# Multiplying x by the norm's weights alone ahead of the hybrid layers' products, and each token's factor into the product's bank

## The chip, the core and the metric

The kernel runs on one core of a Trainium2 chip. The metric is device time in microseconds for one launch, median of several runs. PE is the engine of matrix products, DVE and ACT are the vector and scalar engines, POOL is the general one, and SP issues transfers. A bank is one of the eight accumulators that PE writes, [128 partitions x 512 fp32 values].

## The reference, cut

Two transformer layers with a context stream (the first block) are followed by two hybrid layers, each of which computes, on x of 512 tokens by 1024 features:

```python
def rms_norm(x, g):
    xf = x.astype(jnp.float32)
    y = xf * lax.rsqrt(jnp.mean(xf * xf, axis=-1, keepdims=True) + RMS_EPS)
    return (y * g.astype(jnp.float32)).astype(x.dtype)

def hybrid_layer(x, norm_g, w_in, mla_q_a_norm, mla_w_qb, mla_kv_a_norm, mla_w_kvb,
                 mla_q_norm, mla_k_norm, conv_w, swa_q_norm, swa_k_norm, swa_sinks, w_out):
    h = rms_norm(x, norm_g)
    proj = h @ w_in
    ...
    y_mla = mla_mixer(q_lat, kv_lat, k_rope, mla_q_a_norm, mla_w_qb, mla_kv_a_norm,
                      mla_w_kvb, mla_q_norm, mla_k_norm) * jax.nn.silu(g_mla)
    y_conv = short_conv_mixer(c_h, c_b, c_c, conv_w) * jax.nn.silu(g_conv)
    y_swa = swa_mixer(s_q, s_k, s_v, swa_q_norm, swa_k_norm, swa_sinks) * jax.nn.silu(g_swa)
    y = jnp.concatenate([y_mla, y_conv, y_swa], axis=-1) @ w_out
    return x + y
```

`proj` is split into the query and key-value latents of latent attention (256 and 128 columns) with 32 rotary key columns, the queries, keys and values of a banded attention (512, 128, 128), the three inputs of a short convolution (512 each) and three gates (512 each). The norm's factor `lax.rsqrt(...)` is one number for each token, so `(x * g * r) @ w_in` equals `((x * g) @ w_in) * r`, row by row.

## The kernel before

Activations lie with features on partitions and tokens along the free axis, so a tile of the projection is 128 output columns by 512 tokens in one bank (256 tokens in the context stream). Products are in fp32 by three products of split operands for each 128x128 block of weights: `multiply` does w_hi with x_hi (L367), w_hi with x_lo (L368) and w_lo with x_hi (L369). Eight blocks are a chunk of 512 KB, one transfer. Chunks go through four slots; ACT makes w_hi (L345) and DVE w_lo (L353) two chunks ahead of their use, and a slot is loaded again by SP (L310) when its products are done.

The context stage of layer 0 runs from about 45 to 600 us with 256 tokens; the stages of x follow. Stages are blocks: every engine has a program of its own in each, and the next block begins when all have ended. `rest_stage` (L1318) ends the last layer of the first block: after the MLP's last product, ACT squares x (`square`, L910), PE sums in four lanes (`sum`, L918), DVE gathers the sums out of the bank (`gather`, L924), PE folds them to one number for each token (`fold`, L929), ACT takes the root (`root`, L935). `keep_busy` gives PE idle passes (L476) in that wait. Then `load_stage` (L3312) is a block with SP's loads of the hybrid layers' vectors and late constants alone (L3319).

`hybrid_stage` (L4177) begins with `Lead`: DVE inverts the root (`invert`, L940), PE turns it to rows (`turn`, L945: every partition of a bank holds each token's factor), DVE multiplies x by gain and rows (`scaled`, L1008), ACT makes h_hi (L1000), DVE h_lo (L1020), and PE starts the first two tiles' products, which go through the eight pieces of h side by side. Between the first lead operations ACT and DVE also split two chunks.

`Stream` (L3508) holds the tiles after that: ql0, ql1, kv, kpe, sk (the latents, the rotary keys, the banded keys); the second projections of the latents (q, k, v, from `latent_split`); sv, sq0 to sq3, ch and cc by turns, cb0 to cb3; and gated tiles gs, gm, gc, four each. ACT evicts a tile's bank to SBUF (L3618), or for a gated tile takes a tanh of it (L3612), and then DVE multiplies that with the bank again (L3630). `TokenNorms` (L3651) normalizes heads: ACT squares (L3703), PE sums (L3716), root, inverse, turn (L3747), DVE scales (L3763), and for the latents ACT and DVE make `latent_split` (L3774, L3784). `HybridAttention` (L3868) goes in steps of scores (L3933, L3939), row maxima (DVE, L4033, L4035 and L4030), weights (ACT, L3982), row inverse (L4038), turned weights (PE L3965, ACT L3995) and values (L3951). `ShortConv` (L4066) and `OutPair` (L4134, the first two tiles of the out projection) complete it; the last block adds the out projection to x (L4400) and squares it for the norm that follows.

The order of work on each engine is fixed beforehand: every part is a thread that yields a time of a nominal clock, and `weave_by_clock` (L3480) merges them by that time. A product of a block counts 0.64 us, an attention step 2.0; a tile's eviction is marked at the tile's end, DVE's second pass for a gated tile at end + 0.1. An engine waits at each item for its semaphore, and what is marked later stays behind it.

`Core.take` (L412) and `take_high` place tensors in SBUF: those of 16 KB per partition or more at a multiple of 1024 bytes (`LINE`), others at a multiple of 64. In the context stage h_hi is at 65792 and h_lo at 73984, both 256 beyond a multiple of 1024; mid lies over them; merged_hi and merged_lo are at 118208 and 126400, 448 beyond one. The tensors of 512 tokens are at multiples.

## Time and profile before

| | us |
|---|---|
| median of 3 runs | 3624.76 |
| runs | 3621.72, 3632.71, 3624.76 |
| profiled execution | 3623.7 |
| its span | 3621.8 |
| PE busy in it | 3443.0 |
| DVE, ACT busy | 1907.3, 1391.1 |

The span goes from the first instruction to the last. Times in the rows are microseconds from its start. The granted clock is TensorE's, as a share of full speed (2.4 GHz); its other level is half of that. Of a product of 512 columns the row shows 0.39 us or so at full clock, while the next one starts 0.23 us later: matmuls overlap, and the distance of starts is their cost. An idle time in brackets stands before the instruction of its row, with what ended it.

### The profile page before, as it was taken

The page shows a single profiled execution, that of the slowest core. Times are in us where ns is not written, and L with a number is a line of the kernel's source. Part 1 is how long each engine was busy: PE and PEld are TensorE (multiplying, and loading weights), DVE is VectorE, ACT ScalarE, POOL GpSimd, SP SyncE. Part 2 cuts the span into 40 slices and gives each one's busy share as a digit, 9 for nine tenths or more (in the row PEclk, how much of TensorE's full clock was granted, in tenths as well). Part 3 has the DMA queues.
Part 4 walks back from the last instruction along what each step waited for, and adds up shares of the span by engine and source line. Part 5 has one row for each costly group of instructions (what it writes and reads, how often), then busy time and mean ns, then how long its engine had stood idle before and what let it go on. Part 6 is the DMA issues. An engine that isn't in the chain of part 4 may idle for free. (4 is left out here: it accounts for less than half of the span.)

```text
span 3621.8 us, 46539 instructions
## 1 busy us (share of the span) xinstructions
PE 3443.0 (95%) x18460; PEld 2702.2 (75%) x18460; DVE 1907.3 (53%) x3008; ACT 1391.1 (38%) x2381; POOL 72.8 (2%) x58
## 2 busy tenths in 40 slices
PE   7999999999999999998999999999998999989998
PEld 5878898765777677887775677788875776767767
DVE  4755677946544444455856554454443365343653
ACT  3544443244443322234344443322223344343442
POOL 0000000000000000000000000000000000000000
PEclk8999999999999999999999999999998999999999
DMA  5555454211123643334221122223322211222112
GB/s 195 198 196 194 146 185 150 70 59 41 53 65 105 233 159 120 104 94 137 71 70 41 47 70 93 76 90 97 99 88 83 70 61 43 90 93 65 59 41 99
DMA packets 97258, 366.70 MB, mean 101 GB/s; under 512 B 11168, under 2 KB 11424, under 8 KB 95520
## 3 DMA queue, kind: packets, MB, share of 16 engines
q1 hardware_dynamic: 97056, 363.84, 30.4%
q8 instruction: 147, 2.41, 0.3%
q14 instruction: 55, 0.45, 0.0%
HBM read 354.36 MB, written 9.44 MB: 100 GB/s over the span
## 5 line engine op out<-in xcount | busy, mean ns | idle before, releaser
L353 DVE TENSOR_TENSOR w_lo<-w_raw,w_hi 128x1024 fp32r<-128x1024 f32 x545 | 668.9, 1228 | 606.6 <-ACT w_hi L345 606.4
L367 PE MATMUL banks<-h_hi,w_hi 128*128 128x512 f32 (+1 forms) x1960 | 783.2, 400 | 18.7 <-DVE h_lo L1020 6.4
L369 PE MATMUL banks<-h_hi,w_lo 128*128 128x512 f32 (+1 forms) x1960 | 724.9, 370 | 0.0
L368 PE MATMUL banks<-h_lo,w_hi 128*128 128x512 f32 (+1 forms) x1960 | 723.8, 369 | 0.0
L345 ACT ACTIVATE w_hi<-w_raw 128x1024 fp32r<-128x1024 f32 x545 | 573.5, 1054 | 288.6 <-DMA w_raw<-in_stream 277.1
L367 PEld LDWEIGHTS banks<-h_hi,w_hi 128*128 128x128 f32 x1960 | 375.9, 192 | 120.9 <-issue 57.0
L369 PEld LDWEIGHTS banks<-h_hi,w_lo 128*128 128x128 f32 x1960 | 374.9, 191 | 65.1
L368 PEld LDWEIGHTS banks<-h_lo,w_hi 128*128 128x128 f32 x1960 | 376.8, 192 | 59.2 <-issue 11.1
L367 PE MATMUL banks<-merged_hi,w_hi 128*128 128x512 f32 (+1 forms) x960 | 340.8, 355 | 5.1 <-DVE mid L1663 2.3
L369 PE MATMUL banks<-merged_hi,w_lo 128*128 128x512 f32 (+1 forms) x960 | 337.5, 352 | 0.0
L368 PE MATMUL banks<-merged_lo,w_hi 128*128 128x512 f32 (+1 forms) x960 | 337.5, 352 | 0.0
L367 PE MATMUL banks<-mid_hi,w_hi 128*128 128x512 f32 (+1 forms) x768 | 274.5, 357 | 0.9 <-DVE y L1680 0.5
L369 PE MATMUL banks<-mid_hi,w_lo 128*128 128x512 f32 (+1 forms) x768 | 271.7, 354 | 0.0
L368 PE MATMUL banks<-mid_lo,w_hi 128*128 128x512 f32 (+1 forms) x768 | 271.7, 354 | 0.0
L367 PEld LDWEIGHTS banks<-merged_hi,w_hi 128*128 128x128 f32 x960 | 180.3, 188 | 42.0 <-issue 7.1
L1870 ACT ACTIVATE turned<-banks 128x512 f32<-128x512 f32 (+1 forms) x176 | 96.7, 549 | 283.2 <-PE banks L1849 283.1
L369 PEld LDWEIGHTS banks<-merged_hi,w_lo 128*128 128x128 f32 x960 | 180.3, 188 | 25.3
L368 PEld LDWEIGHTS banks<-merged_lo,w_hi 128*128 128x128 f32 x960 | 180.4, 188 | 24.4
L1594 ACT ACTIVATE mid_hi<-mid 128x512 fp32r<-128x512 f32 (+1 forms) x96 | 54.0, 562 | 309.8 <-DVE mid L1663 309.8
L367 PEld LDWEIGHTS banks<-mid_hi,w_hi 128*128 128x128 f32 x768 | 145.1, 189 | 32.5 <-issue 5.4
L2642 DVE SCALAR_TENSOR_TENSOR branch<-conv_in,vectors,branch 128x512 f32<-128x512 f32 (+1 forms) x270 | 168.1, 670 | 0.2
L369 PEld LDWEIGHTS banks<-mid_hi,w_lo 128*128 128x128 f32 x768 | 145.2, 189 | 20.2
(389 smaller groups left out, 4729.4 us busy)
## 6 DMA issues: line engine op xcount, KB each, us to landing
w_raw<-in_stream SPq DMA_DIRECT2D x545, 512.0 KB, 3.5
mod_cells<-in_stream SPq DMA_DIRECT2D x48, 512.0 KB, 5.4
mod_cell<-in_stream SPq DMA_DIRECT2D x48, 512.0 KB, 5.4
x_kept<-x SPq DMA_DIRECT2D x3, 2048.0 KB, 7.2
x<-x_kept SPq DMA_DIRECT2D x3, 2048.0 KB, 9.9
x<-in_x SPq DMA_DIRECT2D x2, 2048.0 KB, 8.3
out_x<-x SPq DMA_DIRECT2D x8, 256.0 KB, 4.3
dft_table<-in_dft SPq DMA_DIRECT2D x2, 768.0 KB, 5.6
```

What stands on the lines that cost most here:

```text
L345: self.nc.scalar.activation(self.hi[:, c], self.raw[:, c], ACT.Copy).then_inc(self.hi_ready, 1)
L353: self.nc.vector.tensor_tensor(self.lo[:, c], self.raw[:, c], self.hi[:, c].bitcast(F32), ALU.subtract)\
L367: self.nc.tensor.matmul(out, w_hi, x_hi, start=start, stop=False)
L368: self.nc.tensor.matmul(out, w_hi, x_lo, start=False, stop=False)
L369: mm = self.nc.tensor.matmul(out, w_lo, x_hi, start=False, stop=stop)
L1594: nc.scalar.activation(mid_hi[:, t], m[:, t % 2], ACT.Copy).then_inc(mid_hi_ready.sem, 1)
L1870: nc.scalar.activation(self.T[:, lane:lane + lanes, a:b, i * P:(i + 1) * P], K.ps[:, 4, 0:lanes * (b - a) * P].rearrange("p (l k n) -> p l ...
L2642: nc.vector.scalar_tensor_tensor(out=self.out[:, c], in0=src, scalar=w, in1=self.out[:, c], op0=ALU.mult, op1=ALU.add).then_inc(self.done. ...
```

## The change

Ahead of a hybrid layer, `GainLead` takes the place of `Lead`. It multiplies x by the gain only (ACT to hi, DVE to lo), without a wait for the norm's factor. Gather, fold, root, invert and turn are taken out of the end of the stage before and done by the new lead beside the first pair's products: gather first on DVE, fold on PE after piece 0, root on ACT after hi tile 3, invert on DVE after lo tile 4, turn on PE after piece 4. ACT copies the rows to SBUF. Two calls of `keep_busy` go with the fold.

Each tile that uses all eight pieces of h (`raw`) is multiplied on DVE, in its bank, by those rows, at the tile's end; ACT's eviction is marked 0.2 later and waits for that (`normed`), and DVE's second pass of a gated tile is marked 0.3 after the end.

The loads of `load_stage` are issued by SP in the last `rest_stage`, behind its last weight load; the late constants go in space that `branch` gives back early.

`half_skip` is 448 while the context stage is built: split tensors of 8 to 16 KB are then placed 448 beyond a multiple of 1024. With it h_hi is at 65984 and h_lo at 74176; merged stays 448 beyond one, and branch_hi and branch_lo, which were at 448 and 320, come to 448. It is None again for the stages of x.

```diff
--- before.py
+++ after.py
...
     LINE = 1024
+    half_skip = None
...
+    def line_of(self, size, dt):
+        if size >= 16 * self.LINE:
+            return self.LINE, 0
+        if size % self.LINE or size < 8 * self.LINE or self.half_skip is None or dt != F32R:
+            return 64, 0
+        return self.LINE, self.half_skip
+
     def take(self, name, shape, dt=F32):
         size = -(-4 * int(np.prod(shape)) // 64) * 64
-        step = self.LINE if size >= 16 * self.LINE else 64
-        at = -(-self.low // step) * step
+        step, skip = self.line_of(size, dt)
+        at = -(-(self.low - skip) // step) * step + skip
...
+class GainLead:
...
+    def ready(self, pe, k):
+        pe.wait_ge(self.lo_ready.sem, self.lo_ready.at(k + 1))
+
+    def wait_rows(self, eng):
+        eng.wait_ge(self.rows_out.sem, self.rows_out.at(1))
+
+    def pe_beside(self, pe, k):
+        if k == 0:
+            self.norm.fold(pe)
+        elif k == self.n // 2:
+            self.norm.turn(pe)
...
+    def act(self, act, chunks):
+        nc, W = self.K.nc, self.K.W
+        for k in range(self.n):
+            nc.scalar.activation(self.hi[:, k, 0:self.NT], self.src[:, k, 0:self.NT], ACT.Copy, scale=self.gain[:, k:k + 1])\
+                .then_inc(self.hi_ready.sem, 1)
+            if k == self.n // 2 - 1:
+                self.norm.root(act)
+        for c in chunks:
+            W.split_hi(act, c)
+        self.norm.wait_rows(act)
+        nc.scalar.activation(self.rows, self.norm.rows, ACT.Copy).then_inc(self.rows_out.sem, 1)
+
+    def dve(self, dve, chunks):
+        nc, W = self.K.nc, self.K.W
+        self.norm.gather(dve)
+        for k in range(self.n):
+            dve.wait_ge(self.hi_ready.sem, self.hi_ready.at(k + 1))
+            nc.vector.scalar_tensor_tensor(out=self.lo[:, k, 0:self.NT], in0=self.src[:, k, 0:self.NT],
+                                           scalar=self.gain[:, k:k + 1], in1=self.hi[:, k, 0:self.NT].bitcast(F32),
+                                           op0=ALU.mult, op1=ALU.subtract).then_inc(self.lo_ready.sem, 1)
+            if k == self.n // 2:
+                self.norm.invert(dve)
+        for c in chunks:
+            W.split_lo(dve, c)
...
+        @block.sync
+        def _(sp):
+            for dst, src in loads:
+                sp.dma_start(dst, src).then_inc(vectors_in.sem, 16)
+            if loads:
+                sp.wait_ge(vectors_in.sem, vectors_in.at(16 * len(loads)))
...
-                K.keep_busy(pe, busy // 8, 0)
-                following.fold(pe)
...
-                following.root(act)
...
-            if following is not None:
-                following.gather(dve)
...
+        if loads_of is not None:
+            K.give(branch)
...
+        self.normed, self.raw = K.count_of("stream_normed"), [t for t, tile in enumerate(tiles) if len(tile.ks or ()) == KD]
...
-            yield self.end(t)
-            self.wait_done(act, t)
+            yield self.end(t) + (0.2 if t in self.raw else 0.0)
+            if t in self.raw:
+                self.wait_normed(act, t)
+            else:
+                self.wait_done(act, t)
...
+            if t in self.raw:
+                yield self.end(t)
+                if t == self.raw[0]:
+                    self.lead.wait_rows(dve)
+                self.wait_done(dve, t)
+                nc.vector.tensor_tensor(self.out(t), self.out(t), self.lead.rows[0:tile.cols], ALU.mult)\
+                    .then_inc(self.normed.sem, 1)
             if tile.gate:
-                yield self.end(t) + 0.1
+                yield self.end(t) + 0.3
...
+        lead.norm.sq = K.over("lead_squares", temps, F32, [4, NT])
...
-            lead.pe(pe)
             for k in range(KD):
                 lead.ready(pe, k)
                 for t in range(2):
                     W.multiply(pe, K.ps[:, t, 0:NT], first + t * KD + k, h[0][:, k], h[1][:, k], k == 0, k == KD - 1)
+                lead.pe_beside(pe, k)
...
-                following.fold(pe)
...
-            if following is not None:
-                following.root(act)
...
-            lead.dve(dve, lead.squares, range(split - AHEAD, split))
+            lead.dve(dve, range(split - AHEAD, split))
...
-            if following is not None:
-                following.gather(dve)
...
+        hybrid_vectors = []
+
+        def hybrid_loads():
+            K.late_consts = K.take_high("late_consts", [CONST_N - N_EARLY])
+            hybrid_vectors.append(K.take("vectors_2", [2, VEC2_N]))
+            return [(hybrid_vectors[0][:, n], A["vec2"][n]) for n in range(2)] + [(K.late_consts[:], A["consts"][:, N_EARLY:])]
...
+                K.half_skip = 448
...
+            K.half_skip = None
...
-        K.late_consts = K.take("late_consts", [CONST_N - N_EARLY])
...
-        load_stage(K, [(vec2[:, l], A["vec2"][l]) for l in range(2)] + [(K.late_consts[:], A["consts"][:, N_EARLY:])],
-                   "vectors_in")
...
-            lead = Lead(K, before, x, vec[:, VEC2_AT["norm_g"]:VEC2_AT["norm_g"] + 8], None, h[0], h[1], SEQ, False)
+            lead = GainLead(K, before, x, vec[:, VEC2_AT["norm_g"]:VEC2_AT["norm_g"] + 8], h[0], h[1], SEQ)
```

## Rows read from the trace of the kernel before

**Rows 1.** The page: span, and busy time by engine.

```profile
span 3621.8 us, 46539 instructions
...
PE 3443.0 (95%) x18460; PEld 2702.2 (75%) x18460; DVE 1907.3 (53%) x3008; ACT 1391.1 (38%) x2381; POOL 72.8 (2%) x58
```

**Rows 2.** Windows: stretch, length, busy us by engine, TensorE clock, DMA share, GB/s.

```profile
2732.00:2752.00 20.00, 16.58 (x61) 13.54 (x62) 13.43 (x21) 8.19 (x12) 0.00 (x0) 0.73 0.37 135
2946.00:2980.00 34.00, 33.19 (x194) 22.57 (x193) 21.58 (x76) 19.02 (x49) 0.00 (x0) 1.00 0.20 63
3040.00:3070.00 30.00, 27.34 (x171) 20.41 (x168) 16.29 (x35) 13.77 (x33) 0.00 (x0) 1.00 0.12 36
3180.00:3200.00 20.00, 15.93 (x61) 13.07 (x62) 13.46 (x21) 8.51 (x13) 0.00 (x0) 0.75 0.37 134
45.00:150.00 105.00, 98.43 (x764) 93.83 (x764) 83.40 (x166) 55.28 (x102) 4.52 (x6) 0.96 0.44 140
460.00:570.00 110.00, 109.20 (x925) 108.14 (x923) 83.76 (x130) 51.87 (x67) 0.00 (x0) 1.00 0.58 182
```

**Rows 3.** Timeline ahead of hybrid layer 1: start, length, engine, line, operation, idle before.

```profile
2704.91 0.34 SPq L310 DMA_DIRECT2D w_raw<-in_stream  x1
...
2722.75 0.69 DVE L924 COPY squares<-banks 128x512 f32<-128x512 f32 x1 [3.37 <-PE banks L918]
...
2723.49 1.05 PE L929 MATMUL banks<-consts,squares 128*128 128x1 f32 x8 [0.24 <-DVE squares L924]
...
2725.17 0.82 SPq L3319 DMA_DIRECT2D vectors<-in_vec  x2
...
2732.20 2.08 PE L945 MATMUL banks<-consts,norm 128*128 128x128 f32 x8 [7.66 <-DVE norm L940]
...
2735.31 1.40 DVE L1008 SCALAR_TENSOR_TENSOR scaled<-x,vectors,banks 128x512 f32<-128x512 f32 x2
...
2737.49 0.80 PE L367 MATMUL banks<-h_hi,w_hi 128*128 128x512 f32 x1 [3.22 <-DVE h_lo L1020]
```

**Rows 4.** Timeline ahead of hybrid layer 2.

```profile
3176.99 1.28 ACT L935 ACT_TABLE_LOAD   x1
...
3178.16 0.69 DVE L924 COPY squares<-banks 128x512 f32<-128x512 f32 x1 [1.85 <-PE banks L918]
...
3180.60 2.00 ACT L345 ACTIVATE w_hi<-w_raw 128x1024 fp32r<-128x1024 f32 x2 [0.34 <-PEq L4192]
...
3186.15 0.80 PE L367 MATMUL banks<-h_hi,w_hi 128*128 128x512 f32 x1 [3.21 <-DVE h_lo L1020]
```

**Rows 5.** Timeline of PE in the context stage: products on h, then on merged.

```profile
121.52 0.28 PE L367 MATMUL banks<-h_hi,w_hi 128*128 128x256 f32 x1
...
121.88 0.28 PE L367 MATMUL banks<-h_hi,w_hi 128*128 128x256 f32 x1
...
400.01 0.28 PE L367 MATMUL banks<-merged_hi,w_hi 128*128 128x256 f32 x1
...
401.03 0.28 PE L367 MATMUL banks<-merged_hi,w_hi 128*128 128x256 f32 x1
```

**Rows 6.** Timeline of the hybrid layers: pair ends, squares, the out pair.

```profile
2750.58 1.28 ACT L3618 ACTIVATE latents<-banks 128x512 f32<-128x512 f32 x2 [4.77 <-PE banks L369]
...
2756.46 1.78 PE L3716 MATMUL banks<-consts,token_squares 128*128 128x1 f32 x8 [3.88 <-ACT token_squares L3703]
...
2770.00 1.26 PE L3716 MATMUL banks<-consts,token_squares 128*128 128x1 f32 x6 [1.86 <-ACT token_squares L3703]
...
3097.51 0.50 PE L367 MATMUL banks<-swa_out_hi,w_hi 128*128 128x512 f32 x1 [4.11 <-DVE gate_conv L3630]
...
3198.53 1.28 ACT L3618 ACTIVATE latents<-banks 128x512 f32<-128x512 f32 x2 [4.07 <-PE banks L369]
```

**Rows 7.** Instructions of line 4400.

```profile
L4400 DVE TENSOR_TENSOR x<-x,banks x16: 680/686/689, 3124.1 to 3618.6; 128x512 f32<-128x512 f32 x16
```

**Rows 8.** Waits from 2946 to 3102: us in total, times, longest.

```profile
ACT weights L3982 <- DVE neg_max L4035: 30.1, 13, 3.0
```

More of the change, by code:

```diff
@@ L427, in take_high @@
         size = -(-4 * int(np.prod(shape)) // 64) * 64
-        step = self.LINE if size >= 16 * self.LINE else 64
-        at = (self.high - size) // step * step
+        step, skip = self.line_of(size, dt)
+        at = (self.high - size - skip) // step * step + skip
         for a, b, _ in sorted(self.held, key=lambda h: -h[0]):
@@ L432, in take_high @@
                 break
-            at = min(at, (a - size) // step * step)
+            at = min(at, (a - size - skip) // step * step + skip)
         assert at >= self.low, (name, size)
@@ L1315, in close, with rest_stage @@
             self.K.give(t)
-def rest_stage(K, x, merged, mod, mods, NT, following, gates, h, kept, M=None, homes=(), fetch=None, side=None, ahead=None):
+def rest_stage(K, x, merged, mod, mods, NT, following, gates, h, kept, M=None, homes=(), fetch=None, side=None, ahead=None, loads=()):
     nc, W = K.nc, K.W
@@ L1689, in _ @@
                 wait_added(dve, 1, by_pool[-1])
[L1690 to L1691 removed]
+    vectors_in.advance(16 * len(loads))
     residuals = 1 if late_chain else 2
@@ L3453, in block_one_stream @@
     if M is None:
-        late = rest_stage(K, x, merged, mod, mods, NT, after, gates, h, kept, side=side_of() if side_of is not None else None)
+        if loads_of is not None:
+            K.give(branch)
+        late = rest_stage(K, x, merged, mod, mods, NT, after, gates, h, kept, side=side_of() if side_of is not None else None, loads=loads_of() if loads_of is not None else ())
     else:
@@ L3468, in block_one_stream @@
         h = ()
-    for t in (branch, y_hi) + h + merged:
+    for t in ((branch, y_hi) if loads_of is None else (y_hi,)) + h + merged:
         K.give(t)
@@ L3633, in close @@
     def close(self):
-        for s, n in ((self.evicted, len(self.tiles)), (self.gated, len(self.gates)), (self.tile_done, self.done)):
+        for s, n in ((self.evicted, len(self.tiles)), (self.normed, len(self.raw)), (self.gated, len(self.gates)), (self.tile_done, self.done)):
             s.advance(n)
```

28 lines of the change are left out of this document (19 added, 9 removed).

## The prediction, made before the change was built

> **What bounds the kernel now.** The first view is the page's head: PE is busy 3443.0 us of a span of 3621.8, DVE 53% of it, ACT 38% [rows 1]. So PE's products set the time, and an edit pays where it closes a hole in PE's row, or makes a product shorter, and costs where it opens a hole. The profiled execution took 3623.7 us (1.9 around the span) and the median of the runs is 3624.76, 1.1 more; my sum is made on 3623.7. The windows view [rows 2] shows where PE has holes: 3.4 and 4.1 us of 20 at the start of the two hybrid layers (with a granted clock of 0.73 and 0.75), little in the first attention stretch (33.19 of 34), more in a later one (27.34 of 30); in the context stretches PE is busy 94% and 99%. The timeline [rows 3, 4] shows the joints ahead of the hybrid layers, and the waits what the products wait for behind them.
>
> **Part 1: the joint before hybrid layer 1.** DVE gathers the last sums at 2722.75, PE folds at 2723.49, the vectors are loaded from 2725.17, and the next block begins only as they have landed, its turn at 2732.20; two splits, scaled, hi and lo follow, and the first product starts at 2737.49 [rows 3]. After the change the loads are issued behind the last weight load of the stage before (2704.91), 17 us ahead of that gather; SP has nothing queued behind them but its wait for them, and from issue to the next block's first work they took 7.0, so they are covered; were they not, the joint would give up to 7 less. The next block begins about 2723.1 (the sum's arrival at DVE plus the 0.34 that PE's sequencer took at the same joint of layer 2 [rows 4]). A hi tile on ACT and a lo tile on DVE are one operation each on 128x512 from SBUF, for which I take L1008's 0.70; the gather (0.69) runs beside the first hi. First product: 2723.1 + 0.70 + 0.70 = 2724.5, or 13.0 earlier. The four passes of L476 that go lay beside the gather: nothing. The pair of tiles is 48 products. Before they last 2737.49 to 2750.5 [rows 3, 6], 13.0, in which DVE's 1.4 us per k and a low clock are the pace. After, ACT and DVE need 0.70 per k and PE 6 x 0.227 = 1.36 (0.227 being twice the 113.3 ns of 256 columns in [rows 5]), so PE is the pace: 10.9, plus the fold 1.05 and the turn now in its midst, 2.08 at the low clock and half at full: 13.0. The pair ends at 2738.2, with 0.7 for a clock not yet full: 12.3 us gained (11.3 to 13).
>
> **Part 2: the joint before layer 2.** There is no load here. Gather 3178.16, block 3180.60, first product 3186.15, pair's end 3198.53 [rows 4, 6]. After: block 3178.5, first product 3179.9, pair 13.0, and 1.9 more since PE has just idled and the clock is low here before: 3194.8. Gained 3.7 (2.5 to 5). The root's table load (1.28), now beside the sums, falls between ACT's hi tiles 3 and 4, where ACT is 2 us ahead of PE: nothing. Both joints: 16.0.
>
> **Part 3: one multiply more per tile.** 34 tiles in each layer take all 8 pieces of x (5 first ones, sv, 4 sq, 4 ch, 4 cc, 4 cb, 12 gates). Each has its bank multiplied on DVE before ACT may evict it. The like operation is L4400, a TENSOR_TENSOR that adds a bank into 128x512: 0.686 us [rows 7]; with the signal I take 0.74. 34 x 0.74 = 25.2 us of DVE in each layer, and DVE is free 37% and 46% of the two attention stretches [rows 2]; the price is not DVE's time but what waits in ACT's and PE's written-out order. ACT's eviction now stands behind DVE's queue; behind it on ACT stand squares and w_hi splits, and PE waits for the squares' sum.
> - ql pair: PE idles 3.88 for the squares now, which come behind a split that waits for its transfer; the multiply hides under that wait: 0.
> - kv, sk: PE idles 1.86 for kv's squares [rows 6], so nothing covers the delay. kv's multiply stands behind the latents' lo steps on DVE: +1.7; sk +0.75.
> - sv, sq0, ch0, cc0 (the first tile behind another kind): 0.65 to 0.75 each, 2.9 together; sq1, sq2 0.45 together, since norms come later there by the order.
> - cb: the convolution's steps are queued on DVE ahead of the multiply: 1.5 + 1.4 + 0.8, and 0.6 at the first attention step: 4.3.
> Sum 10.1 per layer; I take 9.5 for some overlap, with 5 (only the uncovered ones) and 11 as bounds.
>
> **Part 4: the multiply among the attention.** The 12 gated tiles end while DVE and ACT pass scores to and fro: ACT waits 30.1 us for neg_max in 13 places [rows 8]. A multiply put ahead of a neg_max delays it, ACT's weights, the turn and then PE. By the kernel's own clock the attention goes in steps of 2 us and gated tile t (0 to 11) ends at 5.12 x (t + 1), so its phase in a step is that modulo 2. At phases 0.24 to 0.48 (tiles 1, 3, 10) the multiply is written right ahead of the step's neg_max, and DVE waits there for the tile's last product too: 1.8 each, 5.4. At 0.08, 1.2, 1.36 and 1.84 (tiles 8, 9, 2, 6) it delays the rescaling of weights by its own length or so: 3.2. At the others it falls where DVE waits for ACT: 0. Sum 8.6, an estimate from 0.74 and the order of the code. PE has next to no hole early (0.8 in 34 us) and 2.7 in 30 later, which means the chain has some slack early and none later. I take 8 per layer, bounds 3 (only the later tiles pay) and 10. The gates' second pass (L3630) goes from 0.1 to 0.3 behind the tile's end and has ACT's tanh ahead of it now as before; who needs it (gates, gate_conv) comes later: in the same price. The 4.11 us for which PE waits for gate_conv ahead of the out pair [rows 6] stays: the tanh there stands behind a w_hi split that outlasts the multiply.
>
> **Part 5: the clock.** More holes on PE may mean more stretches at the low clock, as the first products of each layer have. Such a stretch costs about its length less half: I add 1.5 in all (0 to 4).
>
> **Part 6: where h, mid and branch lie in the context stage.** With the skip of 448, h_hi and h_lo of 256 columns move from 256 to 448 beyond a multiple of 1024 bytes, and mid over them as well; merged is at 448 now. Nobody else moves but branch. In the trace products on h_hi start every 120 ns (121.52 to 121.88 in three) and on merged_hi and merged_lo every 113.3 (400.01 to 401.03 in nine), both at full clock, with weight tiles of the same size [rows 5]. 1416 products on h and 768 on mid would gain 2184 x 6.5 ns = 14.2 us, and PE is 94 to 99% busy there [rows 2], and transfers take 0.44 to 0.58 of their engines' time there, so what products lose in length the end mostly gains. I take 12.5; bounds 0 (the gap is due to something else) and 14.5.
> The Trainium skill has a rule that speaks against this part. Its page "TensorE: Matmul & The Clock Gate", section "Wait — 56ns, not 53.3ns?", gives the start-to-start distance as the columns by the clock and about 2.5 ns, and section "Step-by-step: what each phase is for" has cycles by the number of columns alone: where the operand begins isn't in it. By it this part is worth nothing, and the sum would be rival D's. The trace does not agree as it stands, since the two distances above differ at one size and one clock; that placement is the reason is not shown by it.
>
> **Sum.** -16.0 (joints) -12.5 (placement) +2 x (9.5 + 8.0) = +35.0 +1.5 (clock) = +8.0: 3623.7 to 3631.7 profiled, 3632 on the median. What measurement can tell from no change is about 0.3%, 10.9 us: below 3613.9 is faster, above 3635.6 slower.
>
> **The rivals.**
> - A (forecast): gains and costs nearly cancel. 3632, its own range 3621 to 3642.
> - B (slower): the multiply is never covered, since DVE's, ACT's and PE's order is fixed and each tile's eviction hands its delay on. Price 34 x 0.74 = 25.2 per layer, 50.3 in place of 35: -16 -12.5 +50.3 +1.5 = +23.3, 3648. It decides once more than 19.4 us per layer reach PE (26 of the 34 tiles). For it: the kv and sk sums stand bare already. Against: PE's 33.19 of 34 with DVE only 63% busy; where PE is the pace, a later eviction delays nobody.
> - C (faster): DVE's free time takes the multiply except at kv, sk and the first tiles of a kind (5 per layer), and in the attention only the later tiles pay (3): 2 x 8 = 16: -16 -12.5 +16 = -12.5, 3612. For it: early attention is PE's. Against: the 30 us in which ACT waits on DVE.
> - D (the placement does not do it): costs as in A, no gain in the context stage: 3644.5.
> - That the front gains nothing (the loads land late, or the first k waits for the turn after all) I hold below 1 in 20; the code hands PE the first tiles without the norm factor.
>
> **How the numbers follow.** Chances: A 0.52, B 0.12, C 0.26, D 0.10. Faster: half of C, 0.13. Slower: B, four fifths of D and a quarter of A, 0.33. The rest is within 0.3%: 0.54. The range takes all of A, D, most of C and the near part of B: 3610 to 3646.
>
> **What would show it.** The pair's end (ACT's first latents) at about 2738 in place of 2750.58, and about 3.7 gained over the second joint. Products on h_hi at 113 ns in place of 120, and the x stages starting 12 us earlier. PE's hole at kv's sum 3.5 in place of 1.86; each hybrid layer from its pair's end to its last product longer by 17 us. I am wrong if that length grows by under 8 (C) or over 23 (B), or if h stays at 120 (D).

## The result, and the profile after

The changed kernel takes 3659.55 us (median of 5, 3652.36 to 3667.54) against 3624.7 for the kernel before (5 runs): ratio 1.0094, interval 1.0083 to 1.0104. It is 34 us slower, by 0.9%; the forecast was 3632 with a range to 3646. The profiled execution has a span of 3657.8, 36.0 more than [rows 1].

The page of the kernel after, its first lines:

```profile
span 3657.8 us, 46573 instructions
...
PE 3451.7 (94%) x18456; PEld 2700.9 (74%) x18456; DVE 1941.4 (53%) x3060; ACT 1393.1 (38%) x2383; POOL 74.1 (2%) x58
```

PE has 8.7 us more of busy time and 36 more of span. To find where they arise, the products of both kernels (13032 in each, in one order) are set side by side: the start of each tile's first product after, less the same product's start before, and how that difference grows. In both profiled executions:

| from, to | before | after | grows by | forecast |
|---|---|---|---|---|
| start to the first product at 784 (context stage over) | 784.1 | 780.1 | -4.0 | -12.5 |
| to layer 1's first product | 2737.49 | 2720.43 | -13.1 | -13.0 |
| to its kv tile (the pair is done) | 2751.06 | 2736.51 | +2.5 | +0.7 |
| to its gs1 (tiles ahead of the gates) | 2955.74 | 2957.53 | +16.3 | +9.5 |
| to its last product (attention, out projection) | 3175.20 | 3187.24 | +10.3 | +8 |
| to layer 2's first product | 3186.15 | 3192.15 | -6.0 | } -3.7 |
| to its kv tile | 3199.01 | 3208.23 | +3.2 | } |
| to its gs1 | 3400.02 | 3424.99 | +15.8 | +9.5 |
| to its last product | 3618.16 | 3654.13 | +11.0 | +8 |

The sum is +36.0. The joints gave 13.4 and not 16.0, the placement 4.0 and not 12.5, and the layers behind their first pairs took 53.3 more and not 35.0.

The 53.3 are of two kinds. The windows view tells them apart, as PE does the same instructions in both kernels between two such products (stretch, length, busy us of PE, PEld, DVE, ACT, POOL, clock, DMA share, GB/s). Before, the context stage and layer 1 from kv to gs1 and from gs1 to its last product:

```profile
47.95:784.10 736.15, 706.75 (x4995) 622.23 (x4995) 496.66 (x839) 330.50 (x554) 16.73 (x18) 0.99 0.46 152
...
2751.06:2955.74 204.68, 193.12 (x985) 151.18 (x984) 83.32 (x135) 77.67 (x137) 14.59 (x9) 0.96 0.22 68
2955.74:3175.20 219.46, 204.25 (x1141) 151.93 (x1139) 107.06 (x259) 92.65 (x213) 0.00 (x0) 0.99 0.20 65
```

After, the same three:

```profile
48.20:780.10 731.90, 702.26 (x4995) 616.51 (x4995) 496.71 (x839) 330.15 (x554) 17.25 (x18) 0.98 0.47 153
...
2736.51:2957.53 221.02, 198.90 (x985) 153.16 (x984) 97.51 (x157) 78.03 (x137) 15.00 (x9) 0.94 0.20 63
2957.53:3187.24 229.71, 206.17 (x1140) 152.79 (x1139) 114.95 (x271) 93.42 (x213) 0.00 (x0) 0.99 0.19 62
```

From kv to gs1 PE is idle (length less busy) 22.1 us where it was 11.6, and busy 198.90 where it was 193.12, for the same 985 instructions. Over both layers PE's idle time grows by 38.5 us, against 35.0 forecast for the multiplies, and its busy time by 14.8, where the forecast had 1.5 for the clock. The length of a product depends on the granted clock, and one place in layer 1 shows it (before, then after):

```profile
2922.00:2926.00 4.00, 3.79 (x23) 2.99 (x22) 4.00 (x7) 1.38 (x3) 0.00 (x0) 1.00 0.27 104
...
2922.00:2926.00 4.00, 3.81 (x15) 3.18 (x16) 3.22 (x7) 0.40 (x2) 0.00 (x0) 0.63 0.02 4
```

Before, the clock is 1.00 there. After, it is 0.63, products of 512 columns start 0.43 us apart and not 0.23, and PE has just been idle for 2.79 us (timeline, PE):

```profile
2922.19 1.10 PE L3795 MATMUL banks<-consts,token_squares 96*128 96x1 f32 x8 [2.79 <-ACT token_squares L3782]
```

So a hole in PE's row costs its own length, and behind some holes a stretch at the lower clock follows and costs more. Which holes do that is not shown.

In the context stage PE's idle time is the same (29.6 for 29.4) and its busy time 4.5 us shorter.

The timeline of the kernel after ahead of layer 1 answers [rows 3] (start, length, engine, line, operation, idle before it):

```profile
2701.39 0.81 SPq L1462 DMA_DIRECT2D vectors<-in_vec  x2
...
2718.89 0.69 DVE L932 COPY lead_squares<-banks 128x512 f32<-128x512 f32 x1 [3.72 <-PEq L1403]
...
2720.43 0.50 PE L367 MATMUL banks<-h_hi,w_hi 128*128 128x512 f32 x1 [2.01 <-DVE h_lo L1094]
...
2721.73 0.63 PE L369 MATMUL banks<-h_hi,w_lo 128*128 128x512 f32 x1
...
2722.16 1.70 PE L937 MATMUL banks<-consts,lead_squares 128*128 128x1 f32 x8
...
2736.84 1.20 ACT L3690 ACTIVATE latents<-banks 128x512 f32<-128x512 f32 x2 [3.63 <-DVE banks L3704]
```

The loads are out at 2701.39, the block begins at 2718.9 and the first product comes 1.5 later, as forecast. But from 2721.73 the products are longer (0.63 for 0.40), the fold (L937) takes 1.70 in place of 1.05, and PE's clock is low, 0.66 over 2720 to 2730:

```profile
2720.00:2730.00 10.00, 9.57 (x32) 7.91 (x33) 7.56 (x12) 6.03 (x10) 0.00 (x0) 0.66 0.65 238
```

Layer 2's joint, for [rows 4, 6]:

```profile
3192.15 0.50 PE L367 MATMUL banks<-h_hi,w_hi 128*128 128x512 f32 x1 [2.01 <-DVE h_lo L1094]
...
3208.56 1.20 ACT L3690 ACTIVATE latents<-banks 128x512 f32<-128x512 f32 x2 [3.65 <-DVE banks L3704]
```

Measured from the last product of layer 1, the first of layer 2 comes 6.0 sooner than before, and 3.2 are given back while the pair runs, as in layer 1 (2.5).

Who pays for the multiply is told by its own line, all 68 of them (lengths ns, what DVE idled for ahead of it, and who waited for it, us and times):

```profile
L3704 DVE TENSOR_TENSOR banks<-banks,lead_rows x68: 674/694/700, 2736.1 to 3574.5; 128x512 f32<-128x512 f32 x66, 96x512 f32<-96x512 f32 x2
...
  PE banks L369: 42.5, 24
...
  ACT conv_b L3690: 49.7, 8
  ACT swa_q L3690: 40.5, 8
...
  ACT gates L3684: 9.6, 8
```

It lasts 0.694 us against the 0.686 of [rows 7]. DVE stood idle 42.5 us in front of 24 of them until PE had finished the tile, and ACT's evictions stood idle for the multiply: 49.7 us for the 8 of conv_b. Most of that is no price. Before, ACT was idle ahead of the same 8 evictions too, until PE had finished the tile:

```profile
  PE banks L369: 36.6, 8
```

The growth is 13.1 us, 1.6 for each eviction, and 8.4 for the 8 of swa_q (40.5 for 32.1), 1.05 each. Ahead of the gates' tanh, where ACT never idled before, it is 9.6 us now for gates and as much for gate_conv. So an eviction is late by more than the 0.69 of its multiply.

How that reaches PE in the attention is seen at one gate, gs3. Before (timeline, lines of ACT and DVE):

```profile
2986.38 0.58 ACT L3612 ACTIVATE gates<-banks 128x512 f32<-128x512 f32 x1
...
2986.85 1.05 ACT L345 ACTIVATE w_hi<-w_raw 128x1024 fp32r<-128x1024 f32 x1
...
2988.49 0.17 DVE L4030 TENSOR_SCALAR neg_max<-row_max 128x2 f32<-128x2 f32 x1
...
2988.70 0.51 ACT L3982 ACTIVATE weights<-with_bias,neg_max 128x257 f32<-128x257 f32 x1 [0.79 <-DVE neg_max L4030]
...
2989.70 0.57 ACT L3995 ACTIVATE turned<-banks 128x512 f32<-128x512 f32 x1
```

After, the same gate:

```profile
2992.51 0.17 DVE L4109 TENSOR_SCALAR neg_max<-row_max 128x2 f32<-128x2 f32 x1
2992.59 0.69 DVE L3704 TENSOR_TENSOR banks<-banks,lead_rows 128x512 f32<-128x512 f32 x1
...
2992.71 0.51 ACT L4061 ACTIVATE weights<-with_bias,neg_max 128x257 f32<-128x257 f32 x1 [2.23 <-DVE neg_max L4109]
...
2993.71 0.57 ACT L3684 ACTIVATE gates<-banks 128x512 f32<-128x512 f32 x1
...
2994.19 1.04 ACT L345 ACTIVATE w_hi<-w_raw 128x1024 fp32r<-128x1024 f32 x1
...
2995.14 0.58 ACT L4074 ACTIVATE turned<-banks 128x512 f32<-128x512 f32 x1
...
2995.77 0.44 PE L4030 MATMUL banks<-turned,swa_values 128*64 128x128 f32 x4 [0.78 <-ACT turned L4074]
```

Before, ACT waits for DVE's neg_max (the negated row maximum that the weights need) in any case, and does the tanh (L3612) and a w_hi split in that time: 1.6 us for nothing, with 0.79 of idleness left. After, the tanh (L3684) needs the multiply (L3704), which DVE does only behind both with_bias and neg_max. So ACT idles 2.23 ahead of the weights, and the tanh and the split come between the weights and `turned`, on the path: `turned` starts 2.43 behind the weights, where it was 1.00, and PE waits for it. From gm0, in which this falls, to gm1 the difference grows by 1.77.

Distances of products in the context stage, for [rows 5]. On merged, in two stretches of the kernel after:

```profile
359.15 0.28 PE L367 MATMUL banks<-merged_hi,w_hi 128*128 128x256 f32 x1
...
359.86 0.28 PE L367 MATMUL banks<-merged_hi,w_hi 128*128 128x256 f32 x1
...
404.17 0.28 PE L367 MATMUL banks<-merged_hi,w_hi 128*128 128x256 f32 x1
...
404.51 0.28 PE L367 MATMUL banks<-merged_hi,w_hi 128*128 128x256 f32 x1
```

0.71 us for six (118 ns) in the first, 0.34 for three (113) in the second, at one address and one clock. Over the whole stage, of products of 256 columns that follow one another directly at full clock, those on h start every 115.4 ns on average (119.4 before), on mid every 114.0 (119.8) and on merged every 114.3 (113.7). With branch that is 3.0 ns for each of some 3200 products, or 9.6 us.

### The profile page after: what moved, and what is told of

Read it like the earlier page. It is cut to its first block and busy times, and to the rows that moved or that the text cites. A ratio compares the mean times of both kernels' runs of the same rounds, so it can differ in the third digit from the quotient of the medians.

```text
span 3657.8 us, 46573 instructions
## 1 busy us (share of the span) xinstructions
PE 3451.7 (94%) x18456; PEld 2700.9 (74%) x18456; DVE 1941.4 (53%) x3060; ACT 1393.1 (38%) x2383; POOL 74.1 (2%) x58
## 5 line engine op out<-in xcount | busy, mean ns | idle before, releaser
L368 PEld LDWEIGHTS banks<-h_lo,w_hi 128*128 128x128 f32 x1960 | 378.2, 193 | 60.0 <-issue 11.3
```

The lines of the kernel that those rows point to most:

```text
L368: self.nc.tensor.matmul(out, w_hi, x_lo, start=False, stop=False)
```

## The experiments

All times are medians, and the ratios are to runs of the kernel before made beside them (medians of 3626.4 to 3627.0 there). Each edit is shown in part; "..." marks what is left out. From one profiled execution of each kernel, the table gives the growth of the difference to before in the stretches above (B: kv to gs1, C: gs1 to the last product, of layers 1 and 2), and PE's idle time in them, as length less busy time.

| kernel | us | ratio, interval | at kv, layer 1 | B1 | C1 | B2 | C2 | PE idle in B1, C1, B2, C2 |
|---|---|---|---|---|---|---|---|---|
| before | | | 0 | 0 | 0 | 0 | 0 | 11.6, 15.2, 11.3, 15.2 |
| after | 3659.6 | 1.0094 (1.0083 to 1.0104) | -14.6 | 16.3 | 10.3 | 15.8 | 11.0 | 22.1, 23.5, 22.4, 23.6 |
| e1_placement_only | 3620.8 | 0.9983 (0.9973 to 0.9992) | -1.1 | -0.5 | -0.2 | 3.1 | -0.1 | 11.6, 15.3, 11.6, 15.2 |
| e2_no_multiply | 3612.3 | 0.9960 (0.9946 to 0.9974) | -20.9 | -1.7 | 2.1 | 3.7 | 0.7 | 11.5, 15.8, 11.7, 15.8 |
| e3_plain_only | 3646.2 | 1.0051 (1.0034 to 1.0068) | -14.2 | 16.2 | 0.6 | 20.2 | 4.2 | 22.3, 15.8, 22.3, 15.8 |
| e4_one_column | 3646.2 | 1.0049 (1.0032 to 1.0066) | -13.0 | 8.4 | 8.1 | 14.0 | 11.9 | 16.4, 20.7, 16.5, 19.4 |
| e5_loads_placement | 3615.0 | 0.9956 (0.9939 to 0.9972) | -9.4 | -0.1 | 0.1 | 3.2 | 0.0 | 11.5, 15.3, 11.5, 15.2 |
| e6_late_marks | 3671.6 | 1.0121 (1.0104 to 1.0138) | -14.7 | 16.2 | 13.9 | 20.4 | 13.8 | 22.3, 22.7, 22.3, 22.0 |
| e7_pool | 3632.4 | 1.0016 (1.0006 to 1.0025) | -14.3 | -3.5 | 12.9 | 1.9 | 12.0 | 12.6, 22.7, 12.6, 23.6 |
| e8_offset_0 | 3632.3 | 1.0011 (1.0001 to 1.0021) | 11.2 | -0.1 | 0.0 | 0.3 | 0.0 | 11.5, 15.2, 11.6, 15.2 |
| e9_dve_beside | 3622.4 | 0.9992 (0.9982 to 1.0001) | -10.6 | -0.2 | 6.2 | 0.1 | 6.1 | 12.6, 18.7, 12.7, 18.6 |
| e10_act_waits_dve | 3627.0 | 1.0001 (0.9991 to 1.0010) | -14.6 | -1.9 | 10.3 | 5.2 | 8.5 | 12.5, 20.9, 12.7, 20.9 |
| e11_pool_no_gates | 3611.5 | 0.9959 (0.9946 to 0.9972) | -15.1 | 3.1 | 0.6 | 5.1 | 2.3 | 12.6, 15.8, 12.6, 15.8 |
| e12_pool_gates | 3605.2 | 0.9942 (0.9925 to 0.9959) | -13.3 | 2.8 | -3.2 | 5.0 | -3.5 | 12.4, 12.4, 12.6, 12.3 |

The idle time repeats within 0.4 us where kernels have the same work in a stretch (B of before, e1, e2, e5 and e8, both layers of after). The growth does not: with no multiply in B it still moves by 5 us from one execution to another (e2, e5, e11), in steps of about 1.6 at kv, kpe, sk and gs0. These steps are the clock: in B2, e1 is 3.1 us longer than before at 0.3 more of idle time, and its granted clock is 0.96 for 0.97. So the idle time tells the waits, and the rest of the growth is PE's busy time at a lower or higher clock. Over B and C of both layers PE is busy 790 us in before, 790 to 798 in all the kernels in which DVE multiplies no tile outside the gates but kpe, and 805 to 818 in after, e3, e4 and e6, in which it does. So more low clock comes with those multiplies, by more than executions differ. With the gates' alone (e7) it doesn't: 795.

**e1_placement_only.** The placement alone.

```diff
+                K.half_skip = 448
                 late = block_one_stream(K, c, vec, lam[:, l], mod[:, 1], mods[:, 1], CTX, kv_c, [kv_c], None, A["dft256"],
...
+            K.half_skip = None
             x = block_one_stream(K, x, vec, lam[:, l], mod[:, 0], mods[:, 0], SEQ, kv_x, [kv_x, kv_c], A["rope"],
```

> The kernel before, with the placement of the context stage alone (half_skip 448). Theory taken (products get shorter, but part of that is given back in longer waits ahead of products): 4 us faster than before, 3620 to 3622, with products on h and mid starting every 113 to 118 ns. Rival (all that products lose in length the end gains): 8 us or more faster, 3616 or less. Rival (placement does nothing, the 4 us seen by 784 us are chance): within 1 us of before.

3620.8, 6.2 less than before (3 to 10 by the interval): the placement is worth something, and less than the forecast's 12.5. The two ends expected, 4 and 8, both lie in the interval. It is a firmer measure than the -4.0 of one execution: in the twelve profiled kernels with this placement the first product at 784 comes between 9.2 us earlier than before (e2) and 0.4 later (e9), 3.1 earlier on average.

**e8_offset_0.** The same with 0 in place of 448.

```diff
-                K.half_skip = 448
+                K.half_skip = 0
```

> The kernel before with the context stage's split tensors of 8 to 16 KB placed at 0 beyond a multiple of 1024 bytes in place of 448 (merged too, which before was at 448). If the offset alone sets the distance of products: 120 ns or more on h, mid and merged alike, merged 6.7 ns slower than before, and 960 x 6.7 ns = 6.4 us at most to lose: 3627 to 3633. If it is another property of the addresses that made h slow (distance to the weights' slots, or overlap with what others read): h or mid at 114 ns in some stretch, or merged still at 113.

Its timeline of PE, on merged:

```profile
420.00 0.28 PE L367 MATMUL banks<-merged_hi,w_hi 128*128 128x256 f32 x1
...
420.72 0.28 PE L367 MATMUL banks<-merged_hi,w_hi 128*128 128x256 f32 x1
```

0.72 for six: 120 ns, where the same tensor 448 beyond a multiple started every 113.3 in [rows 5]. All through the stage h, mid and merged are at 119 to 120 in this kernel. 3632.3 is 4 to 5 us over before (0 to 8 by the interval), and 6.4 at most was expected. With the h of before (256 beyond) at 120 and of after at 113 to 118, three offsets of the streamed operand are told apart with all else equal: 0 and 256 are slow, 448 is fast. That the offset sets the distance is shown by merged, which moved from 448 to 0 and became slower; why is not shown, and neither is why 448 gives 113 in some stretches and 118 in others.

**e5_loads_placement.** The kernel before with placement and the moved loads, its own `Lead` kept.

```diff
+            for dst, src in loads:
+                sp.dma_start(dst, src).then_inc(vectors_in.sem, 16)
...
-        load_stage(K, [(vec2[:, l], A["vec2"][l]) for l in range(2)] + [(K.late_consts[:], A["consts"][:, N_EARLY:])],
-                   "vectors_in")
```

> The kernel before with the placement and with the loads moved into the last stage of the first block, and with its own Lead, norm and evictions: the parts of the change that add no multiply. Theory: the block that only loads (about 7 us) goes whole, since the loads are covered: 6 + 7 = 13 us faster than before, 3612 to 3616, the first product of hybrid layer 1 starting 7 us earlier and the layers as long as before. Rival (the loads take room in the queue or in SP's order and delay the last stage): 3618 or more.

```profile
2720.27 0.69 DVE L932 COPY squares<-banks 128x512 f32<-128x512 f32 x1 [3.37 <-PE banks L926]
...
2722.71 2.00 ACT L345 ACTIVATE w_hi<-w_raw 128x1024 fp32r<-128x1024 f32 x2 [0.34 <-PEq L1351]
...
2728.26 0.79 PE L367 MATMUL banks<-h_hi,w_hi 128*128 128x512 f32 x1 [3.30 <-DVE h_lo L1028]
```

From gather to first product are 8.0 us here and 14.7 in [rows 3]: 6.7 less, so the loads' block goes whole. 3615.0, 12 under before (10 to 22 by the interval). Of the 13.1 that the changed kernel gains at this joint, 7 are the loads and 6 the new lead, which gives 2.5 back in the pair.

**e2_no_multiply.** The changed kernel with no multiply: both layers lack the norm factor.

```diff
-        self.normed, self.raw = K.count_of("stream_normed"), [t for t, tile in enumerate(tiles) if len(tile.ks or ()) == KD]
+        self.normed, self.raw = K.count_of("stream_normed"), []
```

> The changed kernel with no tile multiplied by the tokens' factor, and evictions waiting for the tile's last product as before: it leaves out the norm factor of both hybrid layers. Theory (the multiply costs all that each layer lost behind its first pair, 26.5 us): 3659.5 - 53 = 3606, and each layer from kv to its last product as long as before. Rival (a part of the loss comes with the new lead itself, its splits and its copy, not with the multiply): 3612 or more, with the loss left ahead of the sk tile.

3612.3: 47 of the 53 go by the medians, at the rival's 3612. But what the rival says, a loss left ahead of sk by the new lead itself, isn't found: PE's idle time in B is that of before (11.5 and 11.7), and only 0.6 in each C is left. The multiply and its waits cause the loss. This kernel is also the most that this lead could give with the places of all else kept, 14.5 us under before, and no better than e5, which keeps the old lead and is complete.

**e3_plain_only.** The multiply at all tiles but the gates, which lack the factor.

```diff
-        self.normed, self.raw = K.count_of("stream_normed"), [t for t, tile in enumerate(tiles) if len(tile.ks or ()) == KD]
+        self.normed, self.raw = K.count_of("stream_normed"), [t for t, tile in enumerate(tiles) if len(tile.ks or ()) == KD and not tile.gate]
```

> The changed kernel with the multiply at the 22 tiles per layer that are not gates, and none at the 12 gated ones: the gates lack the norm factor. If the prices add: 3659.5 - 2 x 11 = 3637.5, with the attention stretch as long as before. If the delay of one part is taken up by the other (a tile that comes late leaves slack for the next): the gain is under 15, 3645 or more.

3646.2, 13.4 less and not 22. In waits the prices add: PE's idle time in C falls to that of e2 (15.8), and in B it stays that of after (22.3). The time doesn't follow in full since the clock differs: C2 is 4.2 and B2 20.2 here, at the same idle time as in e2 and after. So the expectation of 22 and the rival's "under 15" were both about waits; the time lands with the rival, but through the clock.

**e4_one_column.** Each multiply on one column.

```diff
-                nc.vector.tensor_tensor(self.out(t), self.out(t), self.lead.rows[0:tile.cols], ALU.mult)\
+                nc.vector.tensor_tensor(self.out(t)[:, 0:1], self.out(t)[:, 0:1], self.lead.rows[0:tile.cols, 0:1], ALU.mult)\
```

> The changed kernel with each multiply on one column of 512, so that DVE still stands at it until the tile's last product and ACT still waits for it, but it lasts about 0.07 us and not 0.69: it leaves out the factor of 511 tokens. Theory W (the place in DVE's order is the price: DVE is held at the tile's end, and what is written behind it is late): under half of the 53 us go, 3635 or more. Theory D (the 0.69 itself in the chain from tile to eviction is the price): over two thirds go, 3606 to 3622.

```profile
L3704 DVE TENSOR_TENSOR banks<-banks,lead_rows x68: 148/159/168, 2737.7 to 3565.6; 128x1 f32<-128x1 f32 x66, 96x1 f32<-96x1 f32 x2
...
  PE banks L369: 44.5, 25
...
  ACT conv_b L3690: 41.8, 8
  ACT swa_q L3690: 37.0, 8
```

It lasts 0.159 us and not 0.694, yet DVE idles ahead of it as long (44.5). The evictions of conv_b wait 5.2 us more than before (41.8 for 36.6) where it was 13.1, those of swa_q 4.9 (37.0 for 32.1) where it was 8.4. 3646.2: of the 47 us that e2 shows, 13.4 go with the length of the multiply and 34 stay. In PE's idle time half stays: 18.2 us over e2, of 36.8 in after. So the place costs at least as much as the length, and theory D, by which over two thirds would go, falls.

**e6_late_marks.** The gates' multiply, tanh and second pass 1.0 us later in the written order.

```diff
+    def late(self, t):
+        return 1.0 if t in self.gates[:8] else 0.0
```

> The changed kernel with the multiply, the tanh and the second pass of the eight gates gs and gm written 1.0 us of the nominal clock later in the engines' orders; nothing is left out. Theory W (DVE is held at the multiply because it is written where PE has not yet finished the tile): the attention stretch from gs1 to gc0, which lost 5.2 us a layer, loses under 2.5, and the time falls by 5 us or more to 3654 or less. Theory D (the length of the multiply in DVE's row is the price): unchanged within 2 us a layer, since it only moves to another attention step; 3657 to 3662.

3671.6, 10 to 12 us slower still, against 5 or more faster by theory W and no change by theory D. C is 13.9 and 13.8, but not by waits: PE idles 0.8 and 1.6 us less in C than in after, and is busy 4.4 and 4.5 us longer. All of the loss is the clock. So the later marks do shorten the waits a little, as theory W has it, and what they do to the clock outweighs that. Why the clock is lower here isn't shown.

**e7_pool.** No multiply for ql, kv, sk and sq (8 tiles a layer); sv, ch, cc and cb (13) by POOL in SBUF, behind ACT's eviction; kpe and the gates stay on DVE.

```diff
+    def pool(self, pool):
+        for t in self.by_pool:
+            yield self.end(t) + 0.7
...
+            pool.wait_ge(self.evicted.sem, self.evicted.at(t + 1))
+            self.K.nc.gpsimd.tensor_tensor(self.tiles[t].dst, self.tiles[t].dst, self.lead.rows[0:self.tiles[t].cols], ALU.mult)\
+                .then_inc(self.pooled.sem, 1)
```

> The changed kernel with fewer multiplies on DVE: none for ql, kv, sk and sq (what follows normalizes them by their own mean square, and the factor cancels but for its part in epsilon), and for sv, ch, cc and cb ACT evicts as before and POOL multiplies the evicted tile in SBUF. The rotary keys and the gates stay on DVE. Theory W and D both put the loss outside the attention (16 us a layer) in the multiply on DVE: that part goes to under 4 a layer, and the time is 3659.5 - 24 = 3635 or a little less. Rival (a product's factor has to be waited for whichever engine applies it, since PE's sv transposes and DVE's convolution wait for POOL now): half stays, 3645 or more.

One group of POOL's instructions by form (count, busy us, mean ns, idle before):

```profile
L3636 POOL TENSOR_TENSOR conv_b<-conv_b,lead_rows 128x512 f32<-128x512 f32 x8 | 10.3, 1289 | 48.0 <-ACT conv_b L3703 48.0
```

3632.4, 27 less than after. On POOL a multiply takes 1.29 us, nearly twice DVE's, and PE's idle time in B is 12.6, 1.0 over e2, which has no multiply at all. So 13 operations of nearly twice the length cost 1 us a layer where no engine's order holds them up. What the 8 tiles without any multiply save and what POOL saves on the others wasn't tried apart.

**e11_pool_no_gates, e9_dve_beside, e10_act_waits_dve.** Three variants of e7's gates, none of which has the gates' factor. e11 has nothing there. e9 has DVE's stand and work without ACT's wait for it. e10 has ACT's wait for DVE's place, without DVE's stand at the tile's end and with one column of work.

```diff
+                nc.vector.tensor_tensor(self.spare if tile.gate else self.out(t), self.lead.rows if tile.gate else self.out(t), self.lead.rows[0:tile.cols], ALU.mult)\
                     .then_inc(self.normed.sem, 1)
```
```diff
+        if self.tiles[t].gate:
+            self.wait_done(eng, t)
         eng.wait_ge(self.normed.sem, self.normed.at(self.raw.index(t) + 1))
```

(The first is e9's multiply, the second e10's wait ahead of the tanh.)

> The kernel of e7 with no multiply at the twelve gates, which lack the norm factor; it is the base of the next two. If the gates cost 12.5 us a layer, as the attention stretch of e7 shows, 3632 - 25 = 3607, and the attention as long as before.

> The kernel of e7 with the gates' multiply made a side matter: DVE stands at the same place until the tile's last product and then does a multiply of the same size on other data, but ACT's tanh doesn't wait for it; the gates lack the norm factor. Theory H (DVE held at the tile's end, and 0.69 of its row, are the price): 15 us or more of the 25 stay, 3622 or more. Theory L (the price is that ACT's tanh, and all behind it on ACT, waits until DVE has come through its own order, which itself waits for ACT): under 8 us stay, 3615 or less.

> The kernel of e7 with the gates' multiply replaced by one column on other data that doesn't wait for the tile, and ACT's tanh waiting both for the tile's last product and for that place in DVE's order; the gates lack the norm factor. Theory L: 15 us or more of the 25 stay, 3622 or more, since ACT is still tied to DVE's order. Theory H: under 8 us stay, 3615 or less, since DVE isn't held and does no work. If both this and the run beside it keep about half, the price is made of both.

e11 is at 3611.5, so the gates cost 20.9 us in e7. e9 keeps 10.9 of them and e10 15.5, a difference that the medians barely carry. PE's idle time in C does: over e11's 31.6 for both layers it is 5.7 more in e9, 10.2 in e10 and 14.7 in e7. Neither theory has it alone, as each expected under 8 us to stay in the run that keeps the other's part. Tying ACT's tanh to DVE's place (L) brings seven tenths of the waits back with next to no work on DVE, and DVE's stand and work (H) four tenths; the two overlap a little. The timeline of ACT in e10, at a gate, shows the same order as after:

```profile
2973.52 0.51 ACT L4080 ACTIVATE weights<-with_bias,neg_max 128x257 f32<-128x257 f32 x1 [2.23 <-DVE neg_max L4128]
...
2974.53 0.57 ACT L3699 ACTIVATE gates<-banks 128x512 f32<-128x512 f32 x1
...
2975.95 0.58 ACT L4093 ACTIVATE turned<-banks 128x512 f32<-128x512 f32 x1
```

The tanh (L3699) and a split of 1.04 lie between the weights and `turned`.

**e12_pool_gates.** The gates' multiply on POOL as well.

```diff
-                nc.scalar.activation(tile.dst, self.out(t), ACT.Tanh, scale=0.5).then_inc(self.evicted.sem, 1)
+                nc.scalar.activation(tile.dst, self.out(t), ACT.Copy).then_inc(self.evicted.sem, 1)
...
+    def act_tanh(self, act):
+        for g, t in enumerate(self.gates):
+            yield self.end(t) + 1.8
...
+            self.K.nc.scalar.activation(self.spare, self.tiles[t].dst, ACT.Tanh, scale=0.5).then_inc(self.normed.sem, 1)
```

> The kernel of e7 with the gates' multiply on POOL too: ACT copies the gate's bank to SBUF, POOL multiplies it, ACT takes the tanh to a spare tile 1.8 us of the nominal clock after the tile's end, DVE multiplies the two at 2.5; the convolution's gate steps go to 2.6 to 3.2; nothing is left out but epsilon's part in the four kinds of tile named at e7. No engine waits for another's order at the tile's end. 12 more operations of 0.6 us on ACT per layer. Theory L and H: most of the 25 us go, 3610 to 3620. If ACT's added work is on the path: 3621 or more.

```profile
2975.92 0.58 ACT L3695 ACTIVATE gates<-banks 128x512 f32<-128x512 f32 x1
...
2976.40 1.04 ACT L345 ACTIVATE w_hi<-w_raw 128x1024 fp32r<-128x1024 f32 x1
...
2976.58 1.27 POOL L3636 TENSOR_TENSOR gates<-gates,lead_rows 128x512 f32<-128x512 f32 x1 [8.34 <-ACT gates L3695]
...
2979.30 0.51 ACT L4082 ACTIVATE weights<-with_bias,neg_max 128x257 f32<-128x257 f32 x1 [1.86 <-DVE neg_max L4130]
...
2980.30 0.58 ACT L4095 ACTIVATE turned<-banks 128x512 f32<-128x512 f32 x1
```

The copy out of the bank and the split are again in the time in which ACT waits for neg_max; the multiply is on POOL; `turned` (2980.30) starts 1.00 behind the weights, as before. 3605.2, ratio 0.9942 (0.9925 to 0.9959): 21 us under the kernel before and 54 under the changed one, with all work done but epsilon's part in four kinds of tile. C is -3.2 and -3.5, with 2.9 us less of idle time than before in each: the banks come free at the copy and no longer at DVE's second pass, and the out pair starts 2.2 sooner against the tile before it (the wait of 4.11 in [rows 6]). The time is below the 3610 to 3620 expected. This was not foreseen, and its part wasn't tried alone.

## Why the prediction was wrong

The sum for the profiled execution was +8.0 and +36.0 was measured. By its own terms the miss of 28 us is: the clock in the hybrid layers 13.3, the placement 8.5, the multiplies' waits 3.5, the joints 2.6.

**Part 5 is the step that failed most**: "More holes on PE may mean more stretches at the low clock ... I add 1.5 in all (0 to 4)". PE does the same instructions behind the pairs in 14.8 us more of busy time, at a lower granted clock (0.94 for 0.96 from kv to gs1 in layer 1). The forecast took this term from no row. Not all of the 14.8 need be the change's: before is the lowest of ten kernels that lie between 790 and 798 us of busy time there, and after, at 805, is 11 over their mean. The other three kernels with DVE's multiply at the plain tiles lie at 808 to 818.

**Part 3** forecast 9.5 us a layer, bound 11, and PE's idle time grew by 10.6 and 11.1 from kv to gs1. The size is close, and partly by luck. The step "34 x 0.74 = 25.2 ... the price is what waits in ACT's and PE's written-out order" was followed by prices that are each the multiply's own length, once or twice. e4 has a quarter of that length and keeps half of the waits. DVE's place in the written order has to be reached before ACT may evict, and DVE may not go on before PE has finished the tile: two new ties at every tile. The largest excess is from cc3 to gs1, 8.0 us in both layers against 4.3. There conv_b's eviction stands behind DVE's convolution steps and the multiply, ACT's split and squares stand behind the eviction, and PE waits for those squares (L3795) 2.79 and 2.12 us at 2922.19 and 2932.09, where it was 0.21 and 0.79. Behind the first of these holes the clock is low, and the stretch from cb1 to cb2, in which it lies, grows by 4.2: 2.6 by the hole and the rest, about 1.5, behind it.

**Part 4** forecast 8 us a layer, bound 10, and PE's idle time grew by 8.3 and 8.5 behind gs1. By tiles of layer 1 the growth is 1.7 at gs1 and 1.8 at gs3 (1.8 each forecast), 1.2 at gc2 (1.8), and at gs2, gm2, gc0 and gc1 0.6, 0.9, 2.1 and 1.7 (3.2 together). It is 0.3 or less at the others, as forecast, though the forecast for gs0, gm0 and gc3 had no row behind it: their phases, 1.12, 1.6 and 1.44, lie among those that were priced. Of gc0's 2.1, 0.6 comes without a multiply at the gates too (e3, e11). The size was right for a reason that is partly wrong: at gs3 the multiply stands behind neg_max and not ahead of it, and what it delays is ACT's tanh and split, pushed from a time of waiting into the path between weights and `turned` (e10).

**The pair** (Parts 1 and 2, "0.7 for a clock not yet full" and "1.9 more"): PE had idled 2.01 us just before its first product, the clock fell 1.3 us after, and the pair took 16.1 us from its first product to kv's in both layers, where before took 13.6 and 12.9. The joints gave 13.4 where 16.0 were forecast: a term mis-sized by 2.6. This too is the clock, and not the same each time: with the same lead the pair takes 12.9 us in layer 1 of e2 and e10, and 14.2 to 14.5 in layer 2 of six kernels (e2, e3, e6, e7, e11, e12). Up to the first product Part 1 was right: 13.1 gained against 13.0.

**Part 6**: the mechanism was right and its size was off, 4.0 us in this execution and 6.2 alone (e1) for 12.5. First, 6.5 ns for each of 2184 products, 14.2 us, came out as 9.6: h came to 115.4 ns and not 113.3, and merged lost 0.6. Second, the rest was given back through the clock in this execution: 79 products start at the low clock there (213 ns each at 256 columns) where it was 44, and PE's idle time is the same. "PE is 94 to 99% busy there, so what products lose in length the end mostly gains" left the clock out. Waiting takes a part as well: over the twelve profiled kernels with this placement PE idles 31.3 us in the stage on average, 1.9 more than before. Whether shorter products bring more low clock, or this execution of before had little of it, isn't shown.

Rival D falls. The page "TensorE: Matmul & The Clock Gate" of the Trainium skill, section "Wait — 56ns, not 53.3ns?", has the distance of warm products fixed by their columns and about 2.5 ns. The trace doesn't agree: 256 columns come at 113.3, 118 and 120 ns here, the last at offsets 0 and 256.

**The rivals.** The range missed the time by 14 us, and the layers grew by 26.6 and 26.8 us, which the prediction had set as the sign of rival B (over 23). B's 50.3 us for multiplies that are never covered is near the 53.3, but that nearness is luck: the waits are 38.5, nearer to A's 35, and B had the same 1.5 for the clock. (The forecast's 3631.7 and 1.1 make 3632.8, where it says 3632.)

**What stays open**: why 448 is faster than 256, what brings the 118 at one address, which holes bring the low clock, and how much of it is chance.

## What to carry to other kernels

Where every engine runs a fixed order, price an added operation by the ties that it makes, and not by its length alone: list whose order it stands in, what that engine waits for there, and what the engine behind it used to do in that waiting time. Then split a measured loss into the idle time of the engine that sets the pace and its busy time: if the same instructions take longer, the clock is part of the price. If an idle engine can do the operation, let it, even at twice the length, and put its result's reader late. And try the parts of a change one by one: here the moved loads and the placement alone beat the whole.

## What the runs showed of the hardware

A product's streamed operand of 256 columns at an offset of 0 or 256 beyond a multiple of 1024 bytes costs 120 ns, at 448 113.3, or for stretches 118. POOL multiplies 128x512 in SBUF in 1.29 us, DVE out of a bank in 0.69. At the first joint the granted clock fell 1.3 us after PE's restart, with 2.01 us of idleness before it, and was 0.66 over 2720 to 2730. In layer 1 it was 0.63 over 2922 to 2926, behind 2.79 us of idleness, and products of 512 columns started 0.43 us apart there and 0.23 at full clock. From kv to gs1, the same 985 instructions kept PE busy 188.3 us (e9, layer 2) to 199.1 us (e6, layer 2).
